# Two output panels side by side at three stage starts, and filler matmuls while the norm's chain runs

## The reference

```
x = x + mixed @ w_out ; x = rms_norm(x, final_norm_w)          # end of the first block
h = h + 0.5 * rmsnorm(swiglu(rmsnorm(h, n[0]), wi, wo), n[1])  # feed-forward 1
h = h + rmsnorm(hybrid_mixer(rmsnorm(h, n[2]), ...), n[3])     # mixer
h = h + 0.5 * rmsnorm(swiglu(rmsnorm(h, n[4]), wi, wo), n[5])  # feed-forward 2
```

## Time and profile before

| | |
|---|---|
| runs, median (lowest to highest) | 1087.94 us (1087.07 to 1089.46), 3 runs |
| profiled execution, its own time | 1087.07 us |
| its span, first to last instruction | 1085.3 us |
| busy: PE, DVE, ACT, POOL | 94%, 51%, 43%, 70% of the span |
| mean granted PE clock | 0.970 of full speed |
| HBM | 142 GB/s over the span |

### The profile page before, as it was taken

The page is one execution under the profiler, slowest core; times in us unless marked ns, Lnnn a source line. Parts: engine busy times, 40 slices in busy tenths (PEclk is TensorE's granted clock), DMA queues, the critical chain, the costliest instruction groups (busy, mean ns, idle before and its releaser), DMA issues.

```text
span 1085.3 us, 21538 instructions
## 1 busy us (share of the span) xinstructions
PE 1023.1 (94%) x8142; PEld 995.9 (92%) x8142; DVE 549.1 (51%) x1020; ACT 468.7 (43%) x698; POOL 762.6 (70%) x599
## 2 busy tenths in 40 slices
PE   7999999989899999998999899989999889999996
PEld 6899899989899999997898789989999879999995
DVE  4316994455444443335695463445654764445324
ACT  6243224454355444434546434423235364444441
POOL 2496666647859888996578734646629739999994
PEclk9999999999989999998999899989999889999998
DMA  9363333433526555664353122434225526656662
GB/s 351 106 194 117 117 117 117 136 98 117 194 82 184 173 181 159 181 178 152 117 169 107 57 62 94 120 115 126 90 79 172 188 69 194 193 179 185 178 182 70
DMA packets 48297, 154.60 MB, mean 142 GB/s; under 512 B 6028, under 2 KB 11156, under 8 KB 48232
## 3 DMA queue, kind: packets, MB, share of 16 engines
q1 hardware_dynamic: 46080, 151.31, 44.6%
q10 hardware_dynamic: 2152, 2.38, 0.6%
HBM read 151.57 MB, written 2.10 MB: 142 GB/s over the span
## 4 chain that ended last, share of the span: by engine, by line
PE 76%; DVE 12%; issue 4%; POOL 4%; ACT 3%; DMA 0%; SPq 0%; DVEq 0%; ACTq 0%; POOLq 0%
PE panel L1517 59%; PE panel L1561 3%; POOL wlo L591 2%; PE aux L1653 1%; PE panel L1604 1%; DVE qkv L1246 1%; DVE qkv L1251 1%; PE panel L1592 1%; DVE q L1154 1%; DVE s L1133 1%; DVE qkv L1242 1%; DVE k L1155 1%; PE aux L1875 1%; PE aux L1847 1%; PE aux L1838 1%
## 5 line engine op out<-in xcount | busy, mean ns | idle before, releaser
L591 POOL TENSOR_TENSOR wlo<-raw,whi 128x512 fp32r<-128x512 f32 x552 | 733.5, 1360 | 301.2 <-ACT whi L679 299.9
L1517 PE MATMUL panel<-xh,whi 128*128 128x256 f32 (+1 forms) x1504 | 443.5, 295 | 14.5 <-DVE xl L985 9.9
L1517 PE MATMUL panel<-xh,wlo 128*128 128x256 f32 (+1 forms) x1504 | 431.3, 287 | 0.0
L1517 PE MATMUL panel<-xl,whi 128*128 128x256 f32 (+1 forms) x1504 | 430.7, 286 | 0.0
L679 ACT ACTIVATE whi<-raw 128x1024 fp32r<-128x1024 f32 x276 | 286.5, 1053 | 175.0 <-PE panel L1517 152.2
L1517 PEld LDWEIGHTS panel<-xh,whi 128*128 128x128 f32 x1504 | 288.3, 192 | 19.3 <-issue 11.5
L1517 PEld LDWEIGHTS panel<-xl,whi 128*128 128x128 f32 x1504 | 287.4, 191 | 1.6
L1517 PEld LDWEIGHTS panel<-xh,wlo 128*128 128x128 f32 x1504 | 288.0, 191 | 0.0
L1517 PE MATMUL panel<-hh,whi 128*128 128x272 f32 (+1 forms) x352 | 100.1, 284 | 0.0
L1517 PE MATMUL panel<-hh,wlo 128*128 128x272 f32 (+1 forms) x352 | 99.9, 284 | 0.0
L1517 PE MATMUL panel<-hl,whi 128*128 128x272 f32 (+1 forms) x352 | 99.8, 284 | 0.0
(11 more groups left out here) (285 smaller groups left out, 1495.0 us busy)
## 6 DMA issues: line engine op xcount, KB each, us to landing
raw<-in_panels SPq DMA_DIRECT2D x228, 512.0 KB, 3.5
raw<-in_down SPq DMA_DIRECT2D x32, 448.0 KB, 3.3
raw<-in_down SPq DMA_DIRECT2D x16, 512.0 KB, 3.5
memk<-in_mem_panels SPq DMA_DIRECT2D x4, 512.0 KB, 7.4
memv<-in_mem_panels SPq DMA_DIRECT2D x4, 512.0 KB, 13.2
memx<-in_mem SPq DMA_DIRECT2D x4, 256.0 KB, 5.2
h<-in_x SPq DMA_DIRECT2D x1, 1024.0 KB, 8.0
spill<-h ACTq DMA_DIRECT2D x1, 1024.0 KB, 4.7
```

The source lines that it names most:

```text
L591: ins = nc.gpsimd.tensor_tensor(wlo[:, slot, half], raw[:, slot, half], whi[:, slot, half].bitcast(f32), ALU.subtract)
L1517: ins = M(bank[:, 0:w], wt[:, slot, P * t:P * t + P], x[:, kk, c0:c0 + w], start=first and m == 0 and n == 0, stop=last and m == len(pairs ...
```

## The change

Four edits:

- `first_outputs` takes ABREAST = 2 output panels along with each tile: 3 products for the first, 3 for the second, then the matmul of the statistic. The second panel is no longer done after the first. It stands at all three starts; in the mixer the step qkv 1 then has no work of its own on PE.
- `keep_clock` multiplies ones (128x128) by ones into the bank of the next statistic, which that one overwrites later (start=True): 3 times between the two matmuls of `norm_stat`, and 10 (start A) or 13 (B, C) times behind them.
- ACT's split of the fourth panel of a feed-forward (`ahead(UP1_P)`, `ahead(UP2_P)`) moves in front of `post_root`. The old `ahead(UP1_P - 1)` found nothing left to do.
- In ACT's `up_loop` the Silu stands in front of the pair's two `high` and no longer behind them, and the loop handles panels one place further on. Since the loop that follows (the 24 down panels) starts one further too, ACT has split the mixer's fourth panel by the end of feed-forward 1.

```diff
+ABREAST = 2
@@ ACT
             for m in range(4, 16):
                 ahead(WOUT_P + m)
+            ahead(UP1_P)
             post_root(2)
@@ ACT, up_loop
-                        high_in_loop(g, 4, 2 * pair)
-                        high_in_loop(g, 4, 2 * pair + 1)
                         tile = act.snap(g * 2 + pair)
                         act.wait_ge(bank_free[2 * pair], g + (first_o // 4 + 1))
                         A(sil[:, pair, 0:w], sil[:, pair, 0:w], ACT.Silu).then_inc(sil_ready, 1)
+                        high_in_loop(g, 4, 2 * pair)
+                        high_in_loop(g, 4, 2 * pair + 1)
                         act.wait_ge(hid_ready, g * 2 + (layer * FT + pair + 1))
...
-            ahead(UP1_P - 1)
             up_loop(0, UP1_O, LEN)
@@ ACT
                 ahead(OUT2_P + o)
+            ahead(UP2_P)
             nc.scalar.preload_act_table_set(LN_EXP)
             post_root(6)
             pre_norm(7, combined(2), "gains", 32, OUT2_O + 7)
             pre_root(7)
-            ahead(UP2_P - 1)
@@ PE
+            def keep_clock(bank, count):
+
+                for _ in range(count):
+                    M(bank[:, 0:P], ones[:], ones[:], start=True, stop=True)
@@ PE, norm_stat
                 if late:
+                    spare = aux("stat", n + 1) if n < 8 else None
+                    if spare:
+                        aux_open(spare[1])
+                        keep_clock(spare[0], 3)
                     pe.wait_ge(last_squared, n // 2)
                     ins = M(bank[:, 0:W[n]], ones[:], y[:, KT - 1, 0:W[n]], start=False, stop=True)
+                    if spare:
+                        ins.then_inc(aux_full, 1)
+                        keep_clock(spare[0], 10 if n == 2 else 13)
+                        return
@@ PE
-            def first_output(o, p, w, n):
+            def first_outputs(outs, w, n):
...
                 for kk in range(KT):
                     pe.wait_ge(split_low, 8 * SPLIT[n] + kk + 1)
-                    ins = products(pb[o % 4], p % RING, [(kk, kk)], xh, xl, 0, w, kk == 0, kk == KT - 1)
+                    for o, p in outs:
+                        ins = products(pb[o % 4], p % RING, [(kk, kk)], xh, xl, 0, w, kk == 0, kk == KT - 1)
+                        if kk == KT - 1:
+                            ins.then_inc(passed, 1)
                     pe.wait_ge(squared, 8 * SQUARES[n] + kk + 1)
                     total = M(bank[:, 0:w], ones[:], sq[:, kk, 0:w], start=kk == 0, stop=kk == KT - 1)
-                ins.then_inc(passed, 1)
@@ PE, up_loop
-                first_output(first_o, first_p, w, norm)
-                for n in range(1, 4):
+                first_outputs([(first_o + n, first_p + n) for n in range(ABREAST)], w, norm)
+                for n in range(ABREAST, 4):
```

More of the change, by code:

```diff
@@ L1535, in output @@
                 products(pb[o % 4], p % RING, pairs, hi_, lo_, c0, w, True, True, each).then_inc(passed, 1)
-            def first_output(o, p, w, n):
+            def first_outputs(outs, w, n):
                 bank, use = aux("stat", n)
-                open_output(o, p)
+                for o, p in outs:
+                    open_output(o, p)
                 aux_open(use)
@@ L1780, in _ @@
                 if step == ("qkv", 0):
-                    first_output(o, p, LEN, 5)
-                elif kind in ("qkv", "fourier_in", "sconv"):
+                    first_outputs([MIX_OUT[("qkv", n)][0:2] for n in range(ABREAST)], LEN, 5)
+                elif kind in ("qkv", "fourier_in", "sconv") and not (kind == "qkv" and i < ABREAST):
                     output(o, p, xh, xl, LEN)
```

## The result

The changed kernel takes 1081.0 us (median of 8 runs, 1079.15 to 1084.49) against 1087.05 us before (8 runs, 1086.41 to 1089.46). Measured again beside other kernels it came out at 0.9963 (0.9949 to 0.9977), 4 us faster. Both intervals hold the figure that the profile gives for the three starts alone, 5.5 us, the second one just (5.5 of the 1085.73 us that the kernel before took there is a ratio of 0.9949). All ratios here leave out two executions that took several times as long as the others, one of the kernel before (5623.74 us) and one of e5_no_meeting (2568.49 us).

A forecast was written before the change was run, and what follows sets the result against it. PE was taken as the bound, with gains only at the three starts: 1.1 + 0.5 + 1.35 = 2.95, called 3.0 us, off 1087.07 (1084.1) or the median 1087.94 (1084.9), forecast 1084.6 us; range 1081.6 to 1088.4 us.

The forecast's parts named there:

- Bound and tile costs: PE bounds the kernel, gains only at the three starts; a doubled tile takes 1.22 us at full clock.
- Clock: At the three starts filler matmuls keep PE's clock full, cost nothing and leave gaps of about 1.2 to 1.3 us.
- rivals 3 and 4: Filler fails to hold the clock at one start (1086.8 us, chance 0.17) or at all (1091.3 us, chance 0.12).
- Rival 4: At all three starts the filler does not hold the clock: 6.7 us lost, 1091.3 us, chance 0.12.
- after PE had waited most of 3 us: At start A, in the kernel before, the clock was said to fall only after most of a 3 us wait.
- The meeting of POOL and DVE: At each start POOL's moved subtraction holds up DVE's chain: 0.66 us at A, some 0.6 at B and C.
- the sign that was named: In the profile, each chain's first DVE instruction at the starts would take 1.1 us or more instead of 0.45.
- Rival 2: At the starts POOL and DVE meet at no cost, better case at B: 5.2 us won, 1082.4 us, chance 0.23.
- What the starts pass on: Gains left behind the starts: 1.1 us at A, 0.5 at B, 1.35 at C, in all 2.95 us.
- The chain at C is B's: Start C was taken to have the same chain as start B; no separate size was given.
- the rest follows unchanged: Behind the three starts everything just shifts earlier if nothing there absorbs the gain; no size of its own.

The follow-up runs named there:

- e5_no_meeting: Changed kernel with ACT's split of the fourth panel moved between pre_norm and pre_root, and the Ln/Exp table loaded earlier; ratio 0.9959 to the kernel before.
- e1: Changed kernel without any filler matmul, two panels abreast and the ACT changes kept; ratio 0.9993 to the kernel before.
- e2: Kernel before with the filler matmuls added and nothing else; ratio 0.9969 to the kernel before.
- after_again: The changed kernel, unaltered, measured once more beside the other runs; ratio 0.9963 to the kernel before.
- e3: Changed kernel with ACT as before: fourth panel split behind the second root, Silu behind the splits; ratio 1.0027 to the kernel before.
- e6: As e5_no_meeting, but one panel at a time at start A; 1079.55 us, ratio 0.9940 to the kernel before.
- e7: Changed kernel with 5 (A) or 6 (B, C) filler matmuls behind the statistic and none between its halves; ratio 0.9997 to the kernel before.

## Why the prediction was wrong: the sizes, not the mechanisms

**Bound and tile costs: right.** 1.22 us a tile, and 9.7 (A and B) and 9.2 us (C) for two panels were reckoned; measured 1.21 us, and 9.59 at A, 9.87 at B, 8.99 at C. The tiles are no slower at B (1.21 us from one statistic to the next there too): its 9.87 us ends with the first matmul of `wba`, which starts 0.55 us behind the last statistic, where the third panel at A starts 0.26 us behind it.

**Clock: right, but for one reading.** The filler held it (rivals 3 and 4 fell), and e1 shows it is the condition for all else. Rival 4 priced the loss of the clock at 6.7 us, and e1 against the changed kernel measures 6.47. Its 1091.3 us is too high because these 6.7 us were added to a forecast with 3.0 us won where 5.50 were: e1 stands 0.97 us above before in the stretches, and not 3.7. The reading that the clock fell at A "after PE had waited most of 3 us" is wrong: the wait of 2.79 us before 299.24 began at 296.45, and half clock at 297.4, 0.95 us into it; at B and C it began 1.7 and 2.1 us into theirs. No term of the sum rests on it.

**The meeting of POOL and DVE: right at A, too dear at B and C.** Forecast 0.66, 0.58 and 0.58 us; measured, as delay of the first product, 0.59, 0.37 and 0.35. At B the root was late by 0.2 us and DVE's first two took 1.05 instead of 0.91 us, at C it was 0.17 and 0.17 us: DVE came later into POOL's instruction and waited only for what was left of it. So only A shows the sign that was named, a first DVE instruction of 1.1 us. This is 0.5 us of the 2.55 missing. Rival 2 (no cost) fell: moving the split away won 0.60, 0.31 and 0.33 us in e5. That its 5.2 us won lie near the measured 5.50 is luck (its own terms, 2.95 + 1.8 + 0.6, give 5.35).

**"What the starts pass on": the step that failed.** The sum there was 1.1 + 0.5 + 1.35 = 2.95 us, and the stretches show 1.63 + 1.76 + 2.11 = 5.50. All three terms were too small, that of B most.
- At B I took 0.5 us as the middle between two ways for DVE's second tap and POOL's start, 10 ns apart in my reckoning. DVE came first (520.23 against 520.35 us), and one long instruction followed and not two, for which the prediction had 1.1 us. The root came another 0.33 us earlier than reckoned (0.21 of it the cheaper meeting), and DVE took 2.93 us from its first take-in at 519.01 to `ba` where 3.25 were reckoned: together 1.75 us. The rows:

```profile
520.23 0.36 DVE L1242 TENSOR_SCALAR qkv<-pre,vec 128x272 f32<-128x272 f32 x1
520.51 1.50 DVE L1246 SCALAR_TENSOR_TENSOR qkv<-pre,vec,qkv 128x271 f32<-128x271 f32 x1
521.94 0.42 DVE L1262 TENSOR_TENSOR ba<-aux,xrstd 16x272 f32<-16x272 f32 x1
```

```profile
520.35 2.79 POOL L592 TENSOR_TENSOR wlo<-raw,whi 128x512 fp32r<-128x512 f32 x2 [14.76 <-ACT whi L680]
```

  Being late does not change which comes first, since both follow ACT's second root: POOL's subtraction begins 1.34 us behind DVE's first take-in in before (522.60 and 521.26) and here (520.35 and 519.01). The second tap falls 1.22 us behind that take-in, where 1.33 had been reckoned. A mean over two ways that differ by a microsecond is a value that neither has; it makes up 0.6 of the 1.26 us missing at B. It came out alike in both profiles of the changed kernel (20.73 and 20.72 us to `ba`'s transpose).
- At A and C the fifth panel was split earlier than reckoned: a wait of 0.39 us and not 1.0 at A, 0.72 and not 1.3 at C (895.8 against 888.8 and two panels of 2.84). Every link of that chain was one or two tenths shorter: at A the tiles took 9.59 and not 9.7 us, the split began 2.60 us behind the root's start and not 2.71, POOL took 2.54 us and not 2.73; at C the tiles took 8.99 and not 9.2, POOL 2.53. The errors had one sign. With the cheaper meeting they make up the 0.5 us missing at A and the 0.76 at C.

**"The chain at C is B's", "the rest follows unchanged": right.** B's gain reached the first kt 56 us later undiminished (1.76 us at the transpose and at kt), through a part in which the chain that ended last is DVE's from 531 to 568 us.

**The last 0.5 us, and the range.** 5.5 us won from the forecast's base, 1087.5, would be 1082.0 us, inside the range; from the 1087.05 of the comparison it is 1081.5, at its edge. The first comparison gave 1081.0, the second 0.9963, 1083.0 on the same base. What moves is outside the edits: the same code up to A took 290.24 to 294.49 us in ten profiles. Part of that arises before 225 us, with the clock at full in nine of the ten: the same subtraction on POOL starts at 221.71 us in e2 and at 224.28 in e1, for a reason not looked into. The rest goes by the clock between 225 and 262 us: from that subtraction to A it is 68.5 us without half clock (e5), 69.8 to 70.0 with 3.4 us of it (four profiles), 70.8 to 71.4 with 6.8 us (five). The windows of e5_no_meeting, of the changed kernel and of before:

```profile
225.00:262.00 37.00, 31.77 (x236) 1.00 0.35 101
```

```profile
225.00:262.00 37.00, 31.79 (x224) 0.95 0.27 87
```

```profile
225.00:262.00 37.00, 31.60 (x211) 0.91 0.26 88
```

after_again speaks against an effect of the change there: its code is the changed kernel's and it took 294.07. From kt to C the stretch goes by half clock too: 289.7 to 290.5 us with 31 to 34 us of it, 292.3 to 293.2 us with 38 to 41 us. The four profiles without the full filler are all short, and of the six with it four are long (the changed kernel twice, e2 and e3) and two short (e5 and e6); whether the filler or the change draws the kernel to the long side there is not settled.

## What to carry to other kernels

Where PE waits a few microseconds for a chain of other engines between two stages, look at the clock of the stage's first microseconds before making the first products wider: here the wait cost 2 us again behind its end, cheap filler bought that back, and wider work without it bought nothing. Whether a second panel is worth taking along depends on what is slower, the tiles' arrival (at B 1.18 us against PE's 0.84: 1.48 us won, e3 against e2) or PE (at A 0.81 against 0.84: 0.64 us lost, e5 against e6), and it puts off the statistic behind it, so that the next operands must be prepared earlier. Work moved into a quiet place of its own engine is free only if it does not meet another engine's chain there: POOL's subtraction cost DVE's chain 0.59 us at A, and nothing when it came some 10 us later.

## What the runs showed of the hardware

- Ten and thirteen float32 matmuls of ones by ones (128x128, 0.22 us each), with three more ahead, held the granted clock at full across waits that last 3.3 to 3.9 us without them (e1). Five and six of them lost it at two of three starts of one profile (e7: 2.20 and 2.56 us left idle, and half clock of 3.4 us behind each) and held it at the third (2.48 us left).
- Without filler the clock went to half 0.95, 1.7 and 2.1 us into waits of 2.79, 3.61 and 3.55 us (before), and stayed there for 6.8 us each time.
- Waits of 3.26 and 3.41 us between two dense stretches of matmuls (e3) brought half clock for 6.8 us at A and 3.4 us at C; the stretches came out 2.3 and 1.4 us longer than had been expected with the waits alone.
- One DVE instruction with two operands in SBUF (0.48 us) that starts within a POOL instruction ends 0.28 us after it: at A in the changed kernel it began at 295.76 and took 1.07 us, to 296.83, and POOL's had ended at 296.55. At B and C it ended 0.30 and 0.28 us behind POOL's.
